# A two-layer hybrid mixer on one core: three memory panels as rounded passes, state-space powers built eight at a time, sines in another order

## The chip, the cores and the metric

One core of one Trainium2 chip runs the whole program. The metric is the device time of one execution in microseconds. Three runs of the kernel before gave 1199.49, 1192.95 and 1200.73 us, a median of 1199.49 us.

## The reference, cut to what matters

The program is a transformer of two layers over 512 tokens of width 1024. Layer 0 mixes with a gated MLP and a state-space model (S5), layer 1 with an mLSTM and block attention; each layer then has cross attention to a memory of 256 rows and a mixture of 16 experts. The change touches only the first tenth: the keys and values of the memory, and the tables of the state-space model.

```python
# memory keys and values: (256 x 1024) @ (1024 x 2048), once for both layers
memn = rmsnorm(mem, mem_norm_g);  kv = memn @ w_mem_kv
# state-space model: 32 groups, 64 complex states, 16 channels a group
lam_bar = exp(lam * step)
b_bar = ((lam_bar - 1.0) / lam)[..., None] * b_mat
bu = einsum('bsgi,gpi->bsgp', u, b_bar)
_, states = associative_scan(_linear_combine, (lam_bar, bu), axis=1)
y = einsum('bsgp,gip->bsgi', states, c_mat).real
```

The kernel cuts the 512 tokens into chunks of 8. It needs the powers lam_bar^0 to lam_bar^8 times B (the table `s5Qn`, 8 powers) and times C (the table `s5PP`, 9 powers), and rotations by sines and cosines (`s5sin`, `s5cos`) of 64 chunk angles for each of 32 groups.

## The kernel before, in words

All tensors stay on chip as 128 partitions by columns. Each engine has its own hand-written queue of instructions; semaphores order them, and nothing else does. A bank of PSUM is claimed, filled and evacuated by counters.

**Weights** come in panels of 1024 x 512 (2 MB) into two slots of SBUF in turn: kv0 to kv3 for the memory, then ev2, ev1 and ev0 of the mixer. `load_panel` on SP's queue waits until the last product of the slot's previous panel is filled.

**Products of two kinds.** `memory_gemm(n)` (line 894) multiplies in full f32: per panel 2 tiles of rows times 8 steps of k, 16 products of 128 x 128 by 128 x 512; the trace records each as two matmuls. `split_gemm` (line 856) splits each factor into a rounded high part and a low rest (type fp32r) and takes three products, high x high, high x low and low x high: 96 matmuls a panel for 4 row tiles. The parts of the weights go through rings of four tiles, `whi` and `wlo`: for each k, ScalarE copies the 128 x 512 tile to `whi` (line 1481), GpSimd subtracts it from the panel to `wlo` (line 686), TensorE uses both and frees the place (`w_used`).

**The stretch that the change touches** on each engine, in queue order:

- TensorE: memory_gemm(0); transposes of C; memory_gemm(1); 32 transposes of x, which wait for `xn_ready` (`transpose_gain_norm("mix_norm0")`, line 829); memory_gemm(2) and (3); 32 transposes of the table s5Qn (line 917), which wait for `s5_tables` 1; the split product ev2; the products `w` (line 929), which wait for `s5_tables` 2; transposes of the memory keys.
- VectorE: the arguments of exponentials and sines (lines 2098 to 2116), a wait for the sines, the powers' magnitudes (2119, 2120), the mean of x (2123), 13 small operations (2126 to 2135), signs of B and C (2137, 2141), x times its reciprocal root (2154), `combine(BB1)`, the low parts of x (2026), `combine(BB2)`, then 8 and 9 calls of `combine` (2147 to 2149: two multiplications and an addition of 128 x 512 each) for the two tables, then the scaling of the memory keys (2169) and the evacuation of `s5u` (2061).
- ScalarE: squares of the memory, the exponentials (1560 to 1563), squares of x (1504, after x has landed), four sines (1567 to 1570), the root of x, evacuations of kv0 and kv1, the high parts of x (1473), squares of the keys (1583), evacuations of kv2 and kv3, the high parts of the first tiles of ev2 (1481).
- GpSimd: constants, then nothing until the low parts of ev2 (686).

Of the kernel before, what the change touches and what calls it, by code (L numbers as in the profile page):

```python
# [22 lines left out]
F32 = mybir.dt.float32  # L23
# [8 lines left out]
P = 128  # L32
# [44 lines left out]
def program(nc, A, out):  # L77
# [19 lines left out]
    with ctx:  # L97
# [74 lines left out]
        names = """x_in rows_in small_in s5_in lam_in zeros_ready s5_b2 rstd_ready consts_ready mem_rstd wide_in mem_in panel0 panel1 x_hi w_hi w_lo w_used  # L172
        stat_ready if_split hmean_ready hstd_ready mean_ready std_ready xn_ready s5_args s5_exp s5_sin s5_tables s5_w s5_t memk_norm
        ln_mean ln_sq vh_ready ws_masked s5_scan s5_x ya_hi gated ya_lo hd_sq max_ready probs mo_probs last_probs sums_ready wt_second diag_rstd qk_scaled
        a_step d_step p_step qk_ready d_norm ml_args ml_act ml_rows diag_ready dt_ready conv_in hh_sq hh_rstd hh_ready
        spare_rows out_stored xs_stored route_rows y_gathered0 y_gathered1 y_gathered2 y_gathered3
        onehots_ready first_ready late_cols late_onehots late_hi late_lo late_filled xs_rows slots_ready table_ready gate_args gate_exp msum_ready""".split()
# [107 lines left out]
        def await_panel(eng, name):  # L285
# [5 lines left out]

        split_panels = ["ev2", "ev1", "ev0"] + ["out00", "out01"] + \
                       [f"{w}0{n}" for w in ("wq", "wo") for n in range(2)] + [f"od{n}" for n in range(7)] + \
# [144 lines left out]
        memtok = v3(E[0], 2, 2048, 4096)  # L438
        memnT = v3(E[0], 8, 0, 2048)
        memKTf = memKT[:, :, :].rearrange("p a b -> p (a b)")  # L440
        headsel = wsT[0:4, :].rearrange("p (h m) -> p h m", h=4)
# [209 lines left out]
        def _(pool):  # L651
# [29 lines left out]
            def low_parts(*names, k0=0, k1=KT):  # L681
                for name in names:
                    for k in range(k0, k1):
                        s_ = step(name, k)
                        pool.wait_ge(S["w_hi"], s_ + 1)
                        pool.tensor_tensor(wlo[s_ % RING][:, :], slot(name)[:, block_of(name, k), :], whi[s_ % RING][:, :].bitcast(F32),  # L686
                                           ALU.subtract).then_inc(S["w_lo"], 1)

            low_parts("ev2")
            low_parts("ev1", k1=RING)  # L690
# [106 lines left out]
        def _(pe):  # L797
# [88 lines left out]
            def memory_gemm(n):  # L886
                await_panel(pe, f"kv{n}")
                for t in range(MT):
# [7 lines left out]
                    fill(ins, u)  # L896

            memory_gemm(0)

            pe.wait_ge(S["s5_in"], 16 * len(s5_loads))  # L900
            for n, c in enumerate((Cst1, Cst2)):
# [4 lines left out]
                fill(ins, u)  # L906
            memory_gemm(1)
            transpose_gain_norm("mix_norm0")
            memory_gemm(2)
            memory_gemm(3)  # L910

# [22 lines left out]
            u = first["memKT"]  # L934
            pe.wait_ge(S["memk_norm"], 1)
            for k in range(0, KT, 2):
# [86 lines left out]
            pe.wait_ge(S["ws_masked"], 1)  # L1023
            pe.wait_ge(S["vh_ready"], 1)
            for n in range(H):
# [297 lines left out]
            claim(pe, u)  # L1323
            pe.wait_ge(S["diag_rstd"], 1)
            for t in range(TT):
# [4 lines left out]
            claim(pe, u)  # L1330
            pe.wait_ge(S["if_split"], 1)
            for k in range(KT):
# [125 lines left out]
        def _(act):  # L1458
# [98 lines left out]
            act.activation(std[:, 0, 0:MT], ssq[:, 0, 0:MT], ACT.Sqrt).then_inc(S["std_ready"], 1)  # L1557

            act.wait_ge(S["s5_in"], 16 * len(s5_loads))
            act.activation(step_, lstep, ACT.Exp).then_inc(S["s5_exp"], 1)  # L1560
            act.wait_ge(S["s5_args"], 1)
            act.activation(mag, mag, ACT.Exp).then_inc(S["s5_exp"], 1)
            act.activation(rho8, are, ACT.Exp, scale=float(LC)).then_inc(S["s5_exp"], 1)
            squares("mix_norm0")
            act.wait_ge(S["s5_args"], 2)
            act.wait_ge(S["consts_ready"], 2)
            act.activation(Li, Li, ACT.Sin, scale=TWO_PI).then_inc(S["s5_sin"], 1)
            act.activation(Lr, Lr, ACT.Sin, bias=halfpi[:, 0:1], scale=-TWO_PI).then_inc(S["s5_sin"], 1)
            act.activation(s5sin, s5sin, ACT.Sin, scale=TWO_PI).then_inc(S["s5_sin"], 1)
            act.activation(s5cos, s5cos, ACT.Sin, bias=halfpi[:, 0:1], scale=-TWO_PI).then_inc(S["s5_sin"], 1)  # L1570
            root("mix_norm0")

            def mem_rstd(n):
                return rstd[:, 0, n:n + 1]

            act.wait_ge(S["mem_rstd"], 1)
            copies("kv0", 0, 2, lambda n: memtok[:, n, 0:512], scale=mem_rstd)
            copies("kv1", 0, 2, lambda n: memtok[:, n, 512:1024], scale=mem_rstd)
            norm("mix_norm0")
            taken(act, first["kv1"] + 1)  # L1580
            for t in range(MT):
# [422 lines left out]
        def _(dve):  # L2004
# [107 lines left out]
            fraction(Li, Lt)  # L2112
            v(stt(Lr, Li, -1.0, Li, ALU.mult, ALU.max))
            v(tt(s5sin, last(t8, NC), mid(iof[:, 0:NC], G), ALU.mult))
            fraction(s5sin, s5cos)
            v(stt(s5cos, s5sin, -1.0, s5sin, ALU.mult, ALU.max), "s5_args")
# [4 lines left out]
            n0 = NORMS["mix_norm0"]  # L2121
            dve.wait_ge(S["stat_ready"], 2 + 4 * n0)
            v(ts(ssq[:, n0, :], ssq[:, n0, :], 1.0 / D, EPS, ALU.mult, ALU.add), "mean_ready")

            lr1, li1 = Lr[:, :, 1], Li[:, :, 1]
# [5 lines left out]
            for dst, a, b, op in ((Fr, nr, li1, ALU.add), (Fi, li1, nr, ALU.subtract)):  # L2131
                v(tt(n1, a, lamr, ALU.mult))
                v(tt(n2, b, lami, ALU.mult))
                v(tt(n1, n1, n2, op))
                v(tt(dst, n1, th, ALU.mult))
            dve.wait_ge(S["s5_b2"], 32)
            v(ts(B2, B2, nsgn[:, 0:1], None, ALU.mult))
# [7 lines left out]
            def combine(dst, p, a, q, b, op=ALU.add):  # L2145
# [3 lines left out]
                v(tt(dst, tA, tB, op))  # L2149

            dve.wait_ge(S["std_ready"], v.n["mean_ready"])
# [3 lines left out]
            combine(BB1, Fr, B1, Fi, B2)  # L2155
            norm("mix_norm0")
            combine(BB2, Fr, B2, Fi, B1, ALU.subtract)
            for j in range(LC):
                combine(s5Qn[:, :, j, :], Lr[:, :, LC - 1 - j], BB1, Li[:, :, LC - 1 - j], BB2)
# [10 lines left out]
            ins.then_inc(S["memk_norm"], 1)  # L2170

# [51 lines left out]
            dve.wait_ge(S["small_in"], 16 * (len(small) + 1))  # L2223
            tt(Gv, Gv, mid(lngain, 4), ALU.mult).then_inc(S["vh_ready"], 1)
            taken_all(dve, "u0", 4)
# [339 lines left out]
            for t in range(TT):  # L2565
                ins = ts(rstd_diag[:, t * P:(t + 1) * P], ident[:], rstd[:, NORMS["mix_norm1"], t:t + 1], None, ALU.mult)
            ins.then_inc(S["diag_rstd"], 1)
# [7 lines left out]
            dve.nop().then_inc(S["if_split"], 1)  # L2575

# [204 lines left out]
```

## Time and profile before

| | |
|---|---|
| median of three runs | 1199.49 us (1192.95 to 1200.73) |
| profiled execution | span 1194.6 us; the page gives no other time for it |
| TensorE matmul busy | 1161.5 us (97%) |
| TensorE weight loads | 869.9 us (73%) |
| VectorE | 705.1 us (59%) |
| ScalarE | 620.6 us (52%) |
| GpSimd | 373.8 us (31%) |

The span counts from the first to the last instruction of the profiled execution. A busy share is an average over the whole span; the stretch of the change is its first 110 us. In the timeline each line has its start, its duration, engine, source line, operation and count, and in brackets the idle time before it and what ended it.

### The profile page before, as it was taken

Reading aid. Unit: us, or ns where it says so; the run is one execution under the profiler, and the core shown is the slowest. Engines: PE = TensorE matmul, PEld = TensorE weight load, DVE = VectorE, ACT = ScalarE, POOL = GpSimd, SP = SyncE. Lnnn points to the kernel's source line nnn. Section 1 sums busy time; section 2 is a strip of 40 time slices with the busy share of each in tenths; the row PEclk is TensorE's granted clock in tenths of the full one; section 3 lists DMA queues with packets and bytes.
Section 4 is the critical chain, followed back from the end, with each engine's and each line's share of the span. In section 5 each row is a group of like instructions: output and inputs, shape, how many; then the busy total and the mean of one; then the engine's idle time right before and its main releaser. Section 6 shows DMA issues by size and latency. Waiting matters only on the chain.

```text
span 1194.6 us, 15606 instructions
## 1 busy us (share of the span) xinstructions
PE 1161.5 (97%) x5302; PEld 869.9 (73%) x5302; DVE 705.1 (59%) x1267; ACT 620.6 (52%) x1190; POOL 373.8 (31%) x342
## 2 busy tenths in 40 slices
PE   8999999999999899999999999989999998999998
PEld 5468876788778567777778887668887785677776
DVE  4797443332332688888645993682323316888886
ACT  2733245446543467777534354444365524677773
POOL 2034340564223031110635754353442130311113
PEclk9999999999999999999999999999999999999999
DMA  9542232279200989998642221022322009799968
GB/s 295 147 141 79 33 115 72 71 260 373 71 1 5 382 322 390 392 375 322 118 148 80 71 77 65 1 71 71 129 83 72 1 1 386 303 395 382 388 267 186
DMA packets 77644, 213.21 MB, mean 178 GB/s; under 512 B 24039, under 2 KB 24979, under 8 KB 65272
## 3 DMA queue, kind: packets, MB, share of 16 engines
q1 hardware_dynamic: 64688, 180.22, 41.0%
q0 software_dynamic: 10048, 27.20, 7.8%
q10 hardware_dynamic: 2840, 4.91, 1.1%
q8 instruction: 40, 0.66, 0.2%
q14 instruction: 28, 0.23, 0.1%
HBM read 187.90 MB, written 32.51 MB: 185 GB/s over the span
## 4 chain that ended last, share of the span: by engine, by line
PE 82%; DMA 5%; DVE 5%; ACT 4%; issue 2%; SPq 1%; POOL 1%; ACTq 0%; DVEq 0%; POOLq 0%
PE bank L856 39%; PE bank L1222 7%; PE bank L1251 7%; PE bank L1217 6%; PE bank L1076 2%; PE bank L1098 2%; PE bank L894 2%; DMA xs<-E 1%; PE bank L829 1%; PE bank L1037 1%; SPq L613 1%; DMA h<-in_x 1%; DVE E2r L2480 1%; DMA ybuf<-E 1%; ACT E2r L1799 1%
## 5 line engine op out<-in xcount | busy, mean ns | idle before, releaser
L686 POOL TENSOR_TENSOR wlo<-W,whi 128x512 fp32r<-128x512 f32 x176 | 256.7, 1479 | 423.1 <-ACT whi L1481 422.7
L1481 ACT ACTIVATE whi<-W 128x512 fp32r<-128x512 f32 x176 | 108.0, 630 | 244.2 <-PE bank L856 222.9
L856 PE MATMUL bank<-whi,xTr 128*128 128x512 f32 x480 | 193.2, 403 | 1.2 <-ACT E L1967 0.6
L856 PE MATMUL bank<-wlo,xTr 128*128 128x512 f32 x416 | 162.8, 391 | 0.0
L856 PEld LDWEIGHTS bank<-whi,xTr 128*128 128x128 f32 x480 | 90.5, 189 | 22.1 <-POOL wlo L686 2.0
L856 PE MATMUL bank<-whi,E4r 128*128 128x512 f32 x256 | 99.8, 390 | 0.0
L1222 PE MATMUL bank<-E4r,E1r 128*128 128x512 f32 x360 | 98.8, 423 | 0.0
L856 PEld LDWEIGHTS bank<-wlo,xTr 128*128 128x128 f32 x416 | 78.7, 189 | 16.7 <-issue 1.2
L2069 DVE TENSOR_TENSOR h<-bank,h 128x512 f32<-128x512 f32 x32 | 21.8, 691 | 115.0 <-PE bank L856 115.0
L1222 PEld LDWEIGHTS bank<-E4r,E1r 128*128 128x128 f32 x360 | 67.6, 188 | 26.9 <-issue 13.4
L1251 PE MATMUL bank<-whi,E2r 128*128 128x512 f32 x240 | 82.8, 406 | 2.2 <-DVE E2r L2480 0.6
L856 PE MATMUL bank<-whi,E0r 128*128 128x512 f32 x160 | 63.7, 398 | 0.0
L856 PE MATMUL bank<-whi,E2r 128*128 128x512 f32 x160 | 62.4, 390 | 0.0
L856 PE MATMUL bank<-wlo,E0r 128*128 128x512 f32 x160 | 62.2, 389 | 0.0
L720 POOL COPY st<-sm 128x1 f32 x24 | 4.3, 181 | 176.9 <-PE bank L1195 176.9
L1251 PEld LDWEIGHTS bank<-whi,E2r 128*128 128x128 f32 x240 | 45.0, 187 | 18.7 <-DVE E2r L2480 9.8
L894 PE MATMUL bank<-W,E 128*128 128x512 f32 x128 | 57.2, 607 | 0.8 <-DMA W<-in_w_mem_kv 0.8
L856 PEld LDWEIGHTS bank<-whi,E4r 128*128 128x128 f32 x256 | 48.1, 188 | 10.1
L723 POOL DMA_INDIRECT E<-xs,idx x30 | 40.9, 1364 | 26.3 <-POOL idx L721 25.1
L894 PEld LDWEIGHTS bank<-W,E 128*128 128x128 f32 x128 | 24.7, 195 | 31.1 <-issue 30.2
L1251 PE MATMUL bank<-wlo,E2r 128*128 128x512 f32 x120 | 46.8, 390 | 0.0
L1775 ACT ACTIVATE E4r<-W 128x512 fp32r<-128x512 f32 x56 | 33.3, 626 | 23.0 <-DVE sm L2445 18.5
(506 smaller groups left out, 2519.2 us busy)
## 6 DMA issues: line engine op xcount, KB each, us to landing
E<-in_moe_w SPq DMA_DIRECT2D x48, 1024.0 KB, 15.5
W<-in_moe_w SPq DMA_DIRECT2D x32, 1024.0 KB, 11.4
xT<-in_moe_w SPq DMA_DIRECT2D x16, 1024.0 KB, 18.8
W<-in_od_w_in SPq DMA_DIRECT2D x7, 2048.0 KB, 8.5
ybuf<-E SPq DMA_DIRECT2D x26, 512.0 KB, 12.5
ybuf<-memV POOLq DMA_DIRECT2D x12, 1024.0 KB, 19.9
W<-in_w_mem_kv SPq DMA_DIRECT2D x4, 2048.0 KB, 8.9
W<-in_xa_wq SPq DMA_DIRECT2D x4, 2048.0 KB, 8.0
```

Of the source, the lines that this page charges most:

```text
L686: pool.tensor_tensor(wlo[s_ % RING][:, :], slot(name)[:, block_of(name, k), :], whi[s_ % RING][:, :].bitcast(F32), ALU.subtract).then_inc( ...
L723: pool.indirect_dma_start(xg[par], None, xs[l], bass.IndirectOffsetOnAxis(ap=idx[:, par:par + 1], axis=0), bounds_check=T - 1, oob_is_err= ...
L856: ins = pe.matmul(bank(u + t)[:, :], a, b, start=(k == 0 and n == 0), stop=(k == KT - 1 and n == 2))
L894: ins = pe.matmul(bank(u)[:, :], memnT[:, k, t * P:(t + 1) * P], slot(f"kv{n}")[:, k, :], start=(k == 0), stop=(k == KT - 1))
L1076: ins = pe.matmul(bank(u)[:, head * NM:(head + 1) * NM], qT[:, k, t * P:(t + 1) * P], memKT[:, k, :], start=(kk == 0), stop=(kk == 1))
L1098: ins = pe.matmul(bank(u)[:, :], memV[:, k, n * XD + d * P:n * XD + (d + 1) * P], pT[:, n, k, :], start=(k == 0), stop=(k == 1))
L1217: pe.matmul(banks[2 + par][:, :], xgT[:, k, :], w13s[j][:, :, k, :], start=(k == 0), stop=False)
L1222: ins = pe.matmul(banks[2 + par][:, :], a, b, start=False, stop=(c == SPLIT - 1 and n == 2))
L1251: ins = pe.matmul(banks[5 + half][:, :], a, b[:, :], start=(k == 0 and n == 0), stop=(k == 1 and n == 2))
L1481: act.activation(whi[s_ % RING][:, :], slot(name)[:, block_of(name, k), :], ACT.Copy).then_inc(S["w_hi"], 1)
L1775: act.activation(up_hi[c].rearrange("p (n f) -> p n f", n=2), w13s[nj][:, :, KT - SPLIT + c, :], ACT.Copy)\
L2069: evac(tt(hs, bank(u)[:, :], hs, ALU.add), u)
```

## The change

It does five things.

1. Panels kv1, kv2 and kv3 are multiplied as three rounded passes (`memory_split`): 48 matmuls a panel, in steps of k, through the same rings. kv0 stays as it was. The normed memory is split once: ScalarE copies 128 x 2048 to `mem_hi`, GpSimd subtracts to `mem_lo`. Both lie in the buffer E5, where s5PP is built later.
2. ScalarE's queue gets the 24 high parts of these panels between its other work, and GpSimd's queue the 24 low parts ahead of those of ev2.
3. The tables: `combine_eight` builds eight powers with three operations of 128 x 4096 in place of 24 of 128 x 512; the ninth power of s5PP stays a `combine`. The second call waits until kv3's banks are filled.
4. The powers' sines come right after their arguments. The rotation's arguments (`s5sin`, `s5cos`) are finished by VectorE after the 13 small operations, and ScalarE takes their sines after the evacuations of `bT`.
5. VectorE takes the mean of x after the signs of B and C, and `combine(BB1)` before the scaling of x. Some semaphores are merged (`even_setup`, `odd_setup`), with the same order of waits.

```diff
-        split_panels = ["ev2", "ev1", "ev0"] + ["out00", "out01"] + \
+        split_panels = ["kv1", "kv2", "kv3", "ev2", "ev1", "ev0"] + ["out00", "out01"] + \
...
+        mem_hi, mem_lo = v3(E5r, 8, 0, 2048), v3(E5r, 8, 2048, 4096)
...
-            low_parts("ev2")
+            pool.wait_ge(S["mem_hi"], 1)
+            pool.tensor_tensor(mem_lo, memnT, mem_hi.bitcast(F32), ALU.subtract).then_inc(S["mem_lo"], 1)
+            low_parts("kv1", "kv2", "kv3", "ev2")
...
+            def memory_split(n):
+                for k in range(KT):
+                    s_ = step(f"kv{n}", k)
+                    pe.wait_ge(S["w_lo"], s_ + 1)
+                    wh, wl = whi[s_ % RING], wlo[s_ % RING]
+                    for t in range(MT):
...
+                        for i, (a, b) in enumerate(((mem_hi[:, k, c], wh), (mem_hi[:, k, c], wl), (mem_lo[:, k, c], wh))):
+                            ins = pe.matmul(bank(u)[:, :], a, b[:, :], start=(k == 0 and i == 0),
+                                            stop=(k == KT - 1 and i == 2))
...
+                    if k < KT - 1:
+                        ins.then_inc(S["w_used"], 1)
...
-            memory_gemm(1)
+            pe.wait_ge(S["mem_lo"], 1)
+            memory_split(1)
             transpose_gain_norm("mix_norm0")
-            memory_gemm(2)
-            memory_gemm(3)
+            memory_split(2)
+            memory_split(3)
...
+            act.activation(mem_hi, memnT, ACT.Copy).then_inc(S["mem_hi"], 1)
             act.wait_ge(S["s5_in"], 16 * len(s5_loads))
             act.activation(step_, lstep, ACT.Exp).then_inc(S["s5_exp"], 1)
...
-            squares("mix_norm0")
...
+            weights("kv1", 0, RING)
+            act.wait_ge(S["mem_rstd"], 1)
+            copies("kv0", 0, 2, lambda n: memtok[:, n, 0:512], scale=mem_rstd)
+            squares("mix_norm0", 0, 2)
+            weights("kv1", RING, RING + 2)
+            squares("mix_norm0", 2, 4)
+            weights("kv1", RING + 2, KT)
+            root("mix_norm0")
+            weights("kv2", 0, RING - 1)
+            copies("kv1", 0, 2, lambda n: memtok[:, n, 512:1024], scale=mem_rstd)
+            weights("kv2", RING - 1, RING)
+            norm("mix_norm0")
+            weights("kv2", RING, RING + 1)
+            taken(act, first["kv1"] + 1)
+            weights("kv2", RING + 1, RING + 2)
+            memory_key_squares(0)
+            weights("kv2", RING + 2, RING + 3)
+            memory_key_squares(1)
+            weights("kv2", RING + 3, KT)
+            weights("kv3", 0, RING)
             copies("kv2", 0, 2, lambda n: memV[:, n, 0:512], scale=mem_rstd)
-            weights("ev2", 0, RING)
+            weights_between("kv3", "ev2")
             copies("kv3", 0, 2, lambda n: memV[:, n, 512:1024], scale=mem_rstd)
...
+            act.wait_ge(S["s5_args"], 3)
+            act.activation(s5sin, s5sin, ACT.Sin, scale=TWO_PI).then_inc(S["s5_sin"], 1)
+            act.activation(s5cos, s5cos, ACT.Sin, bias=halfpi[:, 0:1], scale=-TWO_PI).then_inc(S["s5_sin"], 1)
...
+            def combine_eight(dst, p, a, q, b):
+                def over_eight(x):
+                    return x.unsqueeze(2).broadcast_to([P, G, LC, GI])
+                product = hflat.rearrange("p (g j i) -> p g j i", g=G, j=LC)
+                tt(dst, last(p, GI), over_eight(a), ALU.mult)
+                v(tt(product, last(q, GI), over_eight(b), ALU.mult))
+                v(tt(dst, dst, product, ALU.add))
+
+            combine_eight(s5Qn, Lr[:, :, LC - 1::-1], BB1, Li[:, :, LC - 1::-1], BB2)
             dve.nop().then_inc(S["s5_tables"], 1)
-            for k in range(LC + 1):
-                combine(s5PP[:, :, k, :], Lr[:, :, k], C1, Li[:, :, k], C2)
+            for t in range(MT):
+                await_filled(dve, first["kv3"] + t)
+            combine_eight(s5PP[:, :, 0:LC, :], Lr[:, :, 0:LC], C1, Li[:, :, 0:LC], C2)
+            combine(s5PP[:, :, LC, :], Lr[:, :, LC], C1, Li[:, :, LC], C2)
             dve.nop().then_inc(S["s5_tables"], 1)
```

## Rows read from the trace of the kernel before

**Rows 1.** The page, busy time of the engines.

```profile
PE 1161.5 (97%) x5302; PEld 869.9 (73%) x5302; DVE 705.1 (59%) x1267; ACT 620.6 (52%) x1190; POOL 373.8 (31%) x342
```

**Rows 2.** Chain of waits, 0 to 260 us: start, duration in us, engine, output, line.

```profile
46.04 5.05 PE bank L829 x29
51.09 27.47 PE bank L894 x64
78.56 3.49 PE bank L917 x32
82.05 21.82 PE bank L856 x96
...
108.51 3.67 PE bank L929 x32
```

**Rows 3.** Timeline of TensorE, 26 to 52 us: start, duration, in brackets idle time.

```profile
28.47 13.90 PE L894 MATMUL bank<-W,E 128*128 128x512 f32 x32
44.14 0.30 PE L829 MATMUL bank<-ident,h 128*128 128x128 f32 x1 [1.78 <-DVE h L2154]
```

**Rows 4.** Timeline of VectorE, 10 to 48 us.

```profile
17.43 0.19 DVE L2098 TENSOR_TENSOR sm<-sm 128x32 f32<-128x32 f32 x1 [2.34 <-ACT sm L1560]
...
21.02 0.46 DVE L2113 SCALAR_TENSOR_TENSOR memKT<-memKT 128x288 f32<-128x288 f32 x1
21.51 2.29 DVE L2114 TENSOR_TENSOR E<-sm,iof 128x2048 f32<-128x2048 f32 x1
23.84 1.23 DVE L2103 TENSOR_SCALAR E<-E 128x2048 f32<-128x2048 f32 x1
...
37.87 0.19 DVE L2126 TENSOR_SCALAR sm<-memKT 128x32 f32<-128x32 f32 x1
...
41.00 0.49 DVE L2137 TENSOR_SCALAR E<-E,nsgn 128x512 f32<-128x512 f32 x1
...
43.24 2.74 DVE L2154 TENSOR_SCALAR h<-h,rstd 128x1024 f32<-128x1024 f32 x4
```

**Rows 5.** Timeline of ScalarE, 14 to 40 us.

```profile
17.07 0.23 ACT L1560 ACTIVATE sm<-sm 128x32 f32<-128x32 f32 x1 [1.34 <-DMA E<-in_s_c_re]
...
30.11 1.06 ACT L1504 ACTIVATE memV<-h 128x1024 f32<-128x1024 f32 x1 [9.86 <-DMA h<-in_x]
...
36.46 1.89 ACT L1569 ACTIVATE E<-E 128x2048 f32<-128x2048 f32 x1
```

**Rows 6.** Timelines of VectorE and GpSimd, 72 to 101 us.

```profile
72.42 0.68 DVE L2148 TENSOR_TENSOR E<-memKT,E 128x512 f32<-128x512 f32 x1
...
73.86 1.65 DVE L2147 TENSOR_TENSOR E<-memKT,E 128x512 f32<-128x512 f32 x1
...
99.59 1.03 DVE L2017 TENSOR_SCALAR st<-st 128x8 f32<-128x8 f32 x1
...
73.48 6.51 POOL L686 TENSOR_TENSOR wlo<-W,whi 128x512 fp32r<-128x512 f32 x4 [62.14 <-ACT whi L1481]
```

**Rows 7.** Timelines of VectorE and GpSimd, 141 to 155 us; last row: line 686, min/median/max ns.

```profile
141.14 2.29 DVE L2195 TENSOR_TENSOR h<-h 128x2048 f32<-128x2048 f32 x1
141.43 3.17 POOL L686 TENSOR_TENSOR wlo<-W,whi 128x512 fp32r<-128x512 f32 x1 [3.60 <-ACT whi L1481]
...
145.90 5.21 DVE L2199 TENSOR_TENSOR_SCAN E<-E,h 128x2048 f32<-128x2048 f32 x1
151.15 3.21 DVE L2200 TENSOR_TENSOR h<-E 128x2048 f32<-128x2048 f32 x1
...
L686 POOL TENSOR_TENSOR wlo<-W,whi x176: 1262/1292/5272, 73.5 to 975.1; 128x512 fp32r<-128x512 f32 x176
```

**Rows 8.** The page, DMA issues: size, median us from issue to landing.

```profile
W<-in_w_mem_kv SPq DMA_DIRECT2D x4, 2048.0 KB, 8.9
```

**Rows 9.** Windows of TensorE: stretch, busy (count), granted clock, DMA.

```profile
46.00:48.00 2.00, 1.96 (x10) 0.54 1.05 406
48.00:50.00 2.00, 2.00 (x13) 0.60 1.12 319
```

More of the change, by code:

```diff
@@ L172, in program @@
         names = """x_in rows_in small_in s5_in lam_in zeros_ready s5_b2 rstd_ready consts_ready mem_rstd wide_in mem_in panel0 panel1 x_hi w_hi w_lo w_used
-        stat_ready if_split hmean_ready hstd_ready mean_ready std_ready xn_ready s5_args s5_exp s5_sin s5_tables s5_w s5_t memk_norm
-        ln_mean ln_sq vh_ready ws_masked s5_scan s5_x ya_hi gated ya_lo hd_sq max_ready probs mo_probs last_probs sums_ready wt_second diag_rstd qk_scaled
+        stat_ready hmean_ready hstd_ready mean_ready std_ready xn_ready s5_args s5_exp s5_sin s5_tables s5_w s5_t even_setup
+        ln_mean ln_sq ws_masked s5_scan s5_x ya_hi gated ya_lo hd_sq max_ready probs mo_probs last_probs sums_ready wt_second odd_setup qk_scaled
         a_step d_step p_step qk_ready d_norm ml_args ml_act ml_rows diag_ready dt_ready conv_in hh_sq hh_rstd hh_ready
+        mem_hi mem_lo
         spare_rows out_stored xs_stored route_rows y_gathered0 y_gathered1 y_gathered2 y_gathered3
@@ L896, in memory_gemm @@
                     fill(ins, u)
+            def memory_split(n):
[4 more added lines that the diff above has]
+                    for t in range(MT):
+                        u = first[f"kv{n}"] + t
+                        if k == 0:
+                            claim(pe, u)
+                        c = slice(t * P, (t + 1) * P)
+                        for i, (a, b) in enumerate(((mem_hi[:, k, c], wh), (mem_hi[:, k, c], wl), (mem_lo[:, k, c], wh))):
+                            ins = pe.matmul(bank(u)[:, :], a, b[:, :], start=(k == 0 and i == 0),
+                                            stop=(k == KT - 1 and i == 2))
+                        if k == KT - 1:
+                            fill(ins, u)
+                    if k < KT - 1:
+                        ins.then_inc(S["w_used"], 1)
             memory_gemm(0)
@@ L934, in _ @@
             u = first["memKT"]
-            pe.wait_ge(S["memk_norm"], 1)
+            pe.wait_ge(S["even_setup"], 1)
             for k in range(0, KT, 2):
@@ L1023, in _ @@
             pe.wait_ge(S["ws_masked"], 1)
-            pe.wait_ge(S["vh_ready"], 1)
+            pe.wait_ge(S["even_setup"], 2)
             for n in range(H):
@@ L1323, in _ @@
             claim(pe, u)
-            pe.wait_ge(S["diag_rstd"], 1)
+            pe.wait_ge(S["odd_setup"], 1)
             for t in range(TT):
@@ L1330, in _ @@
             claim(pe, u)
-            pe.wait_ge(S["if_split"], 1)
+            pe.wait_ge(S["odd_setup"], 2)
             for k in range(KT):
@@ L1557, in _ @@
             act.activation(std[:, 0, 0:MT], ssq[:, 0, 0:MT], ACT.Sqrt).then_inc(S["std_ready"], 1)
+            taken(act, first["memT"] + 2)
+            taken(act, first["memT"] + 3)
+            act.activation(mem_hi, memnT, ACT.Copy).then_inc(S["mem_hi"], 1)
             act.wait_ge(S["s5_in"], 16 * len(s5_loads))
@@ L1568, in _, with memory_key_squares @@
             act.activation(Lr, Lr, ACT.Sin, bias=halfpi[:, 0:1], scale=-TWO_PI).then_inc(S["s5_sin"], 1)
-            act.activation(s5sin, s5sin, ACT.Sin, scale=TWO_PI).then_inc(S["s5_sin"], 1)
-            act.activation(s5cos, s5cos, ACT.Sin, bias=halfpi[:, 0:1], scale=-TWO_PI).then_inc(S["s5_sin"], 1)
-            root("mix_norm0")
             def mem_rstd(n):
                 return rstd[:, 0, n:n + 1]
[L1576 to L1581, printed above, removed]
+            def memory_key_squares(t):
                 for n in range(4):
@@ L2112, in _ @@
             fraction(Li, Lt)
-            v(stt(Lr, Li, -1.0, Li, ALU.mult, ALU.max))
+            v(stt(Lr, Li, -1.0, Li, ALU.mult, ALU.max), "s5_args")
             v(tt(s5sin, last(t8, NC), mid(iof[:, 0:NC], G), ALU.mult))
-            fraction(s5sin, s5cos)
-            v(stt(s5cos, s5sin, -1.0, s5sin, ALU.mult, ALU.max), "s5_args")
             dve.wait_ge(S["s5_exp"], 3)
@@ L2120, in _ @@
             v(tt(Li, Li, mag, ALU.mult))
-            n0 = NORMS["mix_norm0"]
-            dve.wait_ge(S["stat_ready"], 2 + 4 * n0)
-            v(ts(ssq[:, n0, :], ssq[:, n0, :], 1.0 / D, EPS, ALU.mult, ALU.add), "mean_ready")
             lr1, li1 = Lr[:, :, 1], Li[:, :, 1]
@@ L2135, in _ @@
                 v(tt(dst, n1, th, ALU.mult))
+            fraction(s5sin, s5cos)
+            v(stt(s5cos, s5sin, -1.0, s5sin, ALU.mult, ALU.max), "s5_args")
             dve.wait_ge(S["s5_b2"], 32)
@@ L2149, in combine @@
                 v(tt(dst, tA, tB, op))
+            n0 = NORMS["mix_norm0"]
+            dve.wait_ge(S["stat_ready"], 2 + 4 * n0)
+            v(ts(ssq[:, n0, :], ssq[:, n0, :], 1.0 / D, EPS, ALU.mult, ALU.add), "mean_ready")
+            combine(BB1, Fr, B1, Fi, B2)
             dve.wait_ge(S["std_ready"], v.n["mean_ready"])
@@ L2154, in _ @@
                 ts(h[:, t, :], h[:, t, :], rstd[:, NORMS["mix_norm0"], t:t + 1], None, ALU.mult).then_inc(S["xn_ready"], 1)
-            combine(BB1, Fr, B1, Fi, B2)
+            combine(BB2, Fr, B2, Fi, B1, ALU.subtract)
             norm("mix_norm0")
-            combine(BB2, Fr, B2, Fi, B1, ALU.subtract)
-            for j in range(LC):
-                combine(s5Qn[:, :, j, :], Lr[:, :, LC - 1 - j], BB1, Li[:, :, LC - 1 - j], BB2)
+            def combine_eight(dst, p, a, q, b):
[6 more added lines that the diff above has]
+            combine_eight(s5Qn, Lr[:, :, LC - 1::-1], BB1, Li[:, :, LC - 1::-1], BB2)
             dve.nop().then_inc(S["s5_tables"], 1)
-            for k in range(LC + 1):
-                combine(s5PP[:, :, k, :], Lr[:, :, k], C1, Li[:, :, k], C2)
+            for t in range(MT):
+                await_filled(dve, first["kv3"] + t)
+            combine_eight(s5PP[:, :, 0:LC, :], Lr[:, :, 0:LC], C1, Li[:, :, 0:LC], C2)
+            combine(s5PP[:, :, LC, :], Lr[:, :, LC], C1, Li[:, :, LC], C2)
             dve.nop().then_inc(S["s5_tables"], 1)
@@ L2169, in _ @@
                 ins = ts(k, k, xrec[:, n:n + 1], None, ALU.mult)
-            ins.then_inc(S["memk_norm"], 1)
+            ins.then_inc(S["even_setup"], 1)
             copies("s5u", 0, 4, lambda n: uT[:, n, :])
@@ L2223, in _ @@
             dve.wait_ge(S["small_in"], 16 * (len(small) + 1))
-            tt(Gv, Gv, mid(lngain, 4), ALU.mult).then_inc(S["vh_ready"], 1)
+            tt(Gv, Gv, mid(lngain, 4), ALU.mult).then_inc(S["even_setup"], 1)
             taken_all(dve, "u0", 4)
@@ L2566, in _ @@
                 ins = ts(rstd_diag[:, t * P:(t + 1) * P], ident[:], rstd[:, NORMS["mix_norm1"], t:t + 1], None, ALU.mult)
-            ins.then_inc(S["diag_rstd"], 1)
+            ins.then_inc(S["odd_setup"], 1)
             v(dve.memset(VML[:, :, :, P:P + 1], 1.0))
@@ L2574, in _ @@
                 v(tt(iflo[:, :, 32 * n:32 * n + 4], w_, hi_.bitcast(F32), ALU.subtract))
-            dve.nop().then_inc(S["if_split"], 1)
+            dve.nop().then_inc(S["odd_setup"], 1)
             dve.wait_ge(S["rows_in"], 16 * (len(rows_loads) - 1 + len(rope_loads)))
```

## The prediction, made before the changed kernel ran

> **What bounds the kernel now.** I read the page first: TensorE is busy for 97% of the span [rows 1], so a change counts by what it takes from or gives to TensorE's queue. The chain of waits over the first 260 us shows whose work that is here. From 46 us it is TensorE without a gap that matters: transposes of x to 51.1, two full f32 panels in 27.47 us, 32 transposes, and ev2's 96 matmuls in 21.82 us, to 103.9 us [rows 2]. After that it follows TensorE again. What ev2's end moves, the rest of the span moves by.
>
> Before 46 us TensorE's timeline has one idle place: kv1 ends at 42.4, and the transposes wait for VectorE's scaled x, 1.78 us and then piece by piece [rows 3]. VectorE scales x at 43.24 to 45.98 [rows 4], so the chain of small operations ahead of it is the second bound.
>
> The third view is GpSimd against VectorE, because the change gives GpSimd 24 more low parts and a big one. A 128 x 512 operation on VectorE takes 0.68 us alone and 1.65 while GpSimd subtracts, and one of 8 columns then takes 1.03; four low parts take 6.51 us, 1.63 each [rows 6]. So a low part costs VectorE 0.97 us. The reverse is dearer: behind a 2.29 us operation a low part took 3.17 us, and the longest of all, 5272 ns, lies behind the 5.21 us scan, against a median of 1292; the next 128 x 2048 operation then took 3.21 us and not 2.29 [rows 7]. The two engines take strict turns, instruction by instruction.
>
> **The change part by part.**
>
> *Products.* Three passes of 96 matmuls cost 21.82 us [rows 2], 0.227 each; 48 cost 10.9 us against 13.90 for an f32 panel [rows 3]: 3.0 less, 9 us for three. A step of k takes 6 x 0.227 = 1.36 us, and GpSimd alone needs 1.29 (the median) [rows 7], so it just keeps up if VectorE leaves it alone.
>
> *VectorE's chain to scaled x, without GpSimd.* ScalarE's copy to mem_hi costs 1.9 us (as 128 x 2048 sine) [rows 5] and delays the first exponential from 17.07 to 17.7: +0.6. So the powers' arguments end at 22.1 (21.48 before [rows 4]). Then the s5sin product 2.3, two multiplications 1.0, 13 small operations 3.1 (37.87 to 41.00), the rotation's fraction and absolute value 1.23 + 2 x 2.29 = 5.9 with gaps, B and C 2.0 (41.00 to 43.0), the mean 0.2, BB1 2.0, scaling 2.8 [rows 4]: 41.4 us against 45.98. The squares are no limit: x lands at 30.1 [rows 5], four squares and two high parts end near 35.5.
>
> *With GpSimd.* mem_lo is four low parts long. It starts near 16.4 and I take 4 x 1.0 us; VectorE's first operation wants to start at 17.9 and waits: +2.8. The eight low parts of kv1 (panel issued at 15.2, landed near 24 by [rows 8]) fall on the continuous chain, +7.8. The root stands ahead of kv2's high parts in ScalarE's queue, so kv2's first four low parts begin just as BB1 and the scaling run: +3.9. Scaled x is complete at 55.9, 10 us later than before. kv1 ends near 40.5, TensorE idles 15 us, and the transposes end 5.1 us after scaled x (as 45.98 to 51.09), at 61.0.
>
> *kv2 and kv3.* Four tiles are ready, two more come while VectorE reads PSUM (its low parts of x, about 57 to 63; one operand in SBUF). Then BB2 (2.1, plus two turns) to about 66.5, and three operations of 128 x 4096 for s5Qn. Their length is not in the trace: 2 x 2.29 less one fixed part of 0.15 = 4.43 us. Bounds are 4.3 and 5.5 (eight times 0.69). With a low part in each gap it is 3 x 4.43 + 2 x 0.97, to 82. kv2's last two tiles come in those gaps, near 72 and 77, and kv2 ends at 78.7 (64.8 before). kv3's eight low parts find a free port only after s5Qn: 82.7 + 7 x 1.29 + 1.36, kv3 ends at 93.5 against 78.56: +15. The tables' own saving (24 x 0.69 = 16.5 against 13.3) is worth nothing, since TensorE never waited for s5Qn.
>
> *s5PP* now cannot start before kv3 ends. It takes 13.3 + 2.1 + five turns of 0.97 = 20.2, to 114. TensorE has 3.5 us of transposes and ev2 as cover, 97.2 to 119 at best. But ev2's third, fourth and fifth low parts wait out these operations (to about 99.6, 105.0 and 110.4), where TensorE needs one each 2.72 us. That costs it 2.3 us: ev2 ends at 121.3, not 103.87: **+17.4**. The later sines (3.9 us and a table load, in ScalarE's queue ahead of ev2's fifth high part) end near 104.6; ahead of the fifth low part, they hide. So does the panel ev2: issued at kv2's end, landed 9 us later, first used by ScalarE after 90. SP's other loads wait for nothing new. The key squares end before VectorE needs them. The products w then need 8.3 us as before, the keys' scaling being bound by the root behind ev1's fourth high part in both.
>
> The Trainium skill, "SBUF — State Buffer", section "Who interferes with whom", speaks against this change: a VectorE instruction with two SBUF inputs, and a GpSimd one that reads SBUF, hold the shared port for the whole instruction. By it the 4.43 us operations block a low part completely, and the sum stays +17.4; without it the sum would be the second rival's. The 5272 ns row agrees; no row read here has a VectorE operand of 4096 columns.
>
> **Sum.** The profiled span of 1194.6 becomes 1212.0. The median of the runs stood 4.9 us above that span, so 1216.9; I say 1217. With a turn at 0.8 us the same laying out gives +13, at 1.2 us +25.
>
> **Rivals.**
>
> *Half-rate clock.* After the 1.78 us gap the granted clock was 0.54 and 0.60 for four microseconds [rows 9], 1.2 GHz for most of it. After 15 us idle and starved steps in kv2, kv3 may begin at that level: its steps of 1.36 become 2.7 for three or four steps, and the same for ev2's starved start: +4 to +8 on top, 1221 to 1225. For it: such a gap did it here. Against: kv2 and ev2 wait for GpSimd anyway. Chance 0.1.
>
> *No blocking that counts (other side).* If long broadcast operations leave gaps for GpSimd, or the chain's small operations pass it, TensorE sets the pace: scaled x at 41.4, transposes done at 46.4 (-4.7), kv2 and kv3 in 22.4 us and not 27.5 (-5.1): -9.8, ev2 ends at 94 and the median becomes 1189.7. It decides if a low part beside a 4.43 us operation takes under 1.6 us. Against it stand all rows of 6 and 7. A further 3 us could come from the stall before w and full-clock transposes, 1186.5. Chances 0.2 and 0.08.
>
> *Lighter turns.* The turn is 0.5 us, since many of VectorE's operations in the chain are of 0.2 us and GpSimd's read ends before its record: the same laying out gives +7, 1206; +3 to +11 with the big operations at either bound. Chance 0.17.
>
> *mem_lo* could cost four whole median records, 5.2 us [rows 7], and not four turns; another 1.3 us then falls on VectorE, inside the main range.
>
> **How the numbers follow.** The main case (+12 to +22, 1211.5 to 1222) has 0.45, the clock 0.1, lighter turns 0.17, no blocking 0.2, more than that 0.08. One per cent, 12 us, is about what can be told from no change. Slower by over 1%: 0.45 + 0.1 = 0.55. Within: 0.17 + 0.2 = 0.37. Faster: 0.08. The range reaches from the no-blocking case, 1189, to 1224; it leaves out some 0.1 on either side. The main case's own range is 1211 to 1224.
>
> **What would show it.** Low parts (line 686) of 5 to 5.5 us beside the first table's three operations, and again in ev2. VectorE's small operations near 1.2 us where GpSimd works. A first transpose of x behind an idle gap of over 10 us, transposes done near 61, kv3 near 93, ev2 near 121. I am wrong if the low parts stay near 1.3 to 1.6 us throughout, if scaled x is complete before 46, or if kv3 ends before 80.

## The result, and the profile after

The change made the kernel slower: a median of 1213.66 us (4 runs, 1211.61 to 1215.15) against 1197.83 us (4 runs), ratio 1.0163, 95% interval 1.0138 to 1.0188, which is +16.5 to +22.5 us. The four runs of the kernel before taken beside it give only 15.8 us, a quotient of 1.0132 that lies below this interval; the ratio 1.0163 puts the kernel before at 1194.2 us, and its later runs, 7 to 29 at a time, have medians of 1194.0 to 1195.4. I go by the ratio. The profiled execution has a span of 1209.8 us, 15.2 more than before. The page's first line, which answers to [rows 1]:

```profile
PE 1155.5 (96%) x5350; PEld 878.2 (73%) x5350; DVE 710.3 (59%) x1225; ACT 637.9 (53%) x1217; POOL 435.3 (36%) x367
```

TensorE is busy 6 us less and the profiled span is 15 us longer. The chain of waits (start, duration, engine, output, line), which answers to [rows 2]:

```profile
50.45 5.43 DVE h L2195 x4
55.92 5.51 PE bank L833 x29
...
63.63 16.02 POOL wlo L688 x3
79.70 15.53 PE bank L913 x60
...
106.64 5.10 POOL wlo L688
111.88 11.18 PE bank L860 x48
...
128.42 3.67 PE bank L952 x32
...
157.86 19.05 PE bank L860 x84
```

Before, TensorE alone made the chain from 46 us on. Now VectorE's scaling of x takes 5.43 us instead of 2.74 [rows 4] and ends 9.9 us later; the transposes end at 61.4 instead of 51.1; GpSimd's low parts hold the chain for 16 us in kv2 and 5 in ev2; ev2 ends at 123.1 instead of 103.9, and w's second half starts at 128.42 instead of 108.51. I use one mark for every run below: the start of the 84 matmuls of ev1, the first long stretch of products behind everything that the change touches. It is 157.86 here and 137.95 before: +19.9 us.

GpSimd and VectorE beside the first table (timelines, GpSimd's three rows from narrow windows):

```profile
63.63 5.21 POOL L688 TENSOR_TENSOR wlo<-W,whi 128x512 fp32r<-128x512 f32 x1 [8.97 <-ACT whi L1504]
68.81 5.44 POOL L688 TENSOR_TENSOR wlo<-W,whi 128x512 fp32r<-128x512 f32 x1
74.20 5.44 POOL L688 TENSOR_TENSOR wlo<-W,whi 128x512 fp32r<-128x512 f32 x1
...
63.30 4.41 DVE L2205 TENSOR_TENSOR E<-memKT,E 128x4096 f32<-128x4096 f32 x1
67.64 5.49 DVE L2206 TENSOR_TENSOR h<-memKT,E 128x4096 f32<-128x4096 f32 x1
73.16 5.37 DVE L2207 TENSOR_TENSOR E<-E,h 128x4096 f32<-128x4096 f32 x1
```

A *turn* is here the time for which one engine holds the other. Of the 5.2 to 5.4 us of a low part (1.29 us alone) about 1.1 is left once the VectorE operation that it met has ended: the first ends 1.1 us behind the operation of 63.30, and so on. VectorE's next operation is longer by the same turn, 5.49 and 5.37 against 4.41. TensorE's timeline shows who paid, in brackets:

```profile
52.01 0.45 PE L833 MATMUL bank<-ident,h 128*128 128x128 f32 x1 [12.14 <-DVE h L2195]
...
68.89 0.50 PE L913 MATMUL bank<-whi,E5r 128*128 128x512 f32 x1 [1.99 <-POOL wlo L688]
...
74.30 0.79 PE L913 MATMUL bank<-whi,E5r 128*128 128x512 f32 x1 [3.73 <-POOL wlo L688]
...
79.70 0.50 PE L913 MATMUL bank<-whi,E5r 128*128 128x512 f32 x1 [2.48 <-POOL wlo L688]
```

Of the 19.9 us at the mark the profiled span shows 15.2, because the rest of the program was 4.7 us shorter in this execution. Chains of waits, the same two places in the kernel before and, second fence, after:

```profile
303.17 5.46 PE bank L856 x24
...
1181.14 9.08 PE bank L1274 x40
```

```profile
323.06 5.46 PE bank L860 x24
...
1196.41 9.08 PE bank L1297 x40
```

That is 878.0 us between the two rows before and 873.4 after. The same stretch took 873.0, 875.3, 872.5 and 875.7 us in the first four experiments, which share this code: it varies by itself, and before was the longest. Part of the difference in this pair is one panel's transfer, 9.12 against 7.87 us on the chain. So I read nothing as given back; the interval of the repeated runs holds 19.9.

### The profile page after: what moved, and what is told of

It is laid out like the page before. It is cut to its first block, busy times and chain, and to the rows that moved or that the text cites. A ratio compares the mean times of both kernels' runs of the same rounds, so it can differ in the third digit from the quotient of the medians.

```text
span 1209.8 us, 15724 instructions
## 1 busy us (share of the span) xinstructions
PE 1155.5 (96%) x5350; PEld 878.2 (73%) x5350; DVE 710.3 (59%) x1225; ACT 637.9 (53%) x1217; POOL 435.3 (36%) x367
## 4 chain that ended last, share of the span: by engine, by line
PE 80%; DVE 7%; ACT 5%; DMA 4%; POOL 2%; issue 1%; ACTq 0%; DVEq 0%; POOLq 0%
PE bank L860 38%; PE bank L1274 8%; PE bank L1245 8%; PE bank L1240 6%; DMA xs<-E 3%; PE bank L1099 2%; PE bank L1121 2%; POOL wlo L688 2%; PE bank L1297 2%; ACT E L1796 1%; PE bank L913 1%; PE bank L1060 1%; DVE E2r L2532 1%; PE bank L833 1%; ACT E2r L1840 1%
## 5 line engine op out<-in xcount | busy, mean ns | idle before, releaser
L688 POOL TENSOR_TENSOR wlo<-W,whi 128x512 fp32r<-128x512 f32 x200 | 312.4, 1576 | 376.2 <-ACT whi L1504 375.5
L1504 ACT ACTIVATE whi<-W 128x512 fp32r<-128x512 f32 x200 | 122.5, 630 | 250.2 <-PE bank L860 223.1
L860 PEld LDWEIGHTS bank<-wlo,xTr 128*128 128x128 f32 x416 | 78.2, 188 | 16.5 <-issue 1.2
L1274 PE MATMUL bank<-whi,E2r 128*128 128x512 f32 x240 | 82.7, 405 | 2.2 <-DVE E2r L2532 0.6
L727 POOL DMA_INDIRECT E<-xs,idx x30 | 41.4, 1379 | 25.8 <-POOL idx L725 25.8
L1816 ACT ACTIVATE E4r<-W 128x512 fp32r<-128x512 f32 x56 | 33.3, 627 | 21.8 <-DVE sm L2497 17.4
L1240 PE MATMUL bank<-E 128*128 128x512 f32 x96 | 43.8, 592 | 0.0
L2385 DVE TENSOR_TENSOR E<-bank,fgain 128x512 f32<-128x512 f32 x64 | 41.2, 682 | 4.3 <-PE bank L1218 2.1
## 6 DMA issues: line engine op xcount, KB each, us to landing
E<-in_moe_w SPq DMA_DIRECT2D x48, 1024.0 KB, 15.2
xT<-in_moe_w SPq DMA_DIRECT2D x16, 1024.0 KB, 17.4
```

What stands on the lines that cost most here:

```text
L727: pool.indirect_dma_start(xg[par], None, xs[l], bass.IndirectOffsetOnAxis(ap=idx[:, par:par + 1], axis=0), bounds_check=T - 1, oob_is_err= ...
L860: ins = pe.matmul(bank(u + t)[:, :], a, b, start=(k == 0 and n == 0), stop=(k == KT - 1 and n == 2))
L1240: pe.matmul(banks[2 + par][:, :], xgT[:, k, :], w13s[j][:, :, k, :], start=(k == 0), stop=False)
L1274: ins = pe.matmul(banks[5 + half][:, :], a, b[:, :], start=(k == 0 and n == 0), stop=(k == 1 and n == 2))
L1504: act.activation(whi[s_ % RING][:, :], slot(name)[:, block_of(name, k), :], ACT.Copy).then_inc(S["w_hi"], 1)
L1816: act.activation(up_hi[c].rearrange("p (n f) -> p n f", n=2), w13s[nj][:, :, KT - SPLIT + c, :], ACT.Copy)\
```

## The experiments

The theory, *turns*: a subtraction on GpSimd and a VectorE operation that both read SBUF (two operands, or a scaling of SBUF data) do not overlap. A low part costs VectorE about 1 us; a VectorE operation costs a low part its whole length. A low part is the subtraction that makes the rest of a weight tile. Rivals: the feed of the passes (rings, ScalarE's order), the clock, the new order on VectorE, the long operations alone. Each ratio is to the runs of the kernel before that belong to that experiment (medians 1193.96 to 1195.41). The mark is that of one profiled execution, so it moves with the clock of that execution too.

| run | median us | ratio to before (95%) | mark us |
|---|---|---|---|
| before | 1194 to 1198 | 1 | 137.95 |
| the change | 1213.66 | 1.0163 (1.0138 to 1.0188) | 157.86 |
| no passes | 1190.42 | 0.9975 (0.9946 to 1.0004) | 140.01 |
| single powers | 1214.77 | 1.0168 (1.0136 to 1.0199) | 159.99 |
| GpSimd writes only | 1188.20 | 0.9947 (0.9929 to 0.9964) | 135.31 |
| the order alone | 1186.96 | 0.9942 (0.9926 to 0.9959) | 132.83 |
| s5u evacuated first | 1187.50 | 0.9943 (0.9921 to 0.9964) | 131.60 |
| twelve dummies | 1199.79 | 1.0043 (1.0024 to 1.0062) | 148.27 |
| eight powers alone | 1194.74 | 0.9995 (0.9979 to 1.0011) | 141.89 |
| kv3 alone | 1197.82 | 1.0023 (1.0007 to 1.0039) | 140.62 |
| free chain | 1203.66 | 1.0075 (1.0049 to 1.0101) | 147.85 |

**No passes.**

```diff
-            memory_split(1)
+            memory_gemm(1)
...
-            low_parts("kv1", "kv2", "kv3", "ev2")
+            low_parts("ev2")
...
-            for t in range(MT):
-                await_filled(dve, first["kv3"] + t)
             combine_eight(s5PP[:, :, 0:LC, :], Lr[:, :, 0:LC], C1, Li[:, :, 0:LC], C2)
```

> The change without the rounded passes: kv1 to kv3 as full f32 panels again, no high or low parts for them, no split of the memory; the sines' order, the mean's place and the tables built eight at a time stay, and the second table no longer waits for kv3. Turns theory (each low part takes about 1 us from VectorE, each VectorE operation with two SBUF operands holds a low part back for its whole length): the loss is gone, scaled x is complete near 40, the transposes start when kv1 ends (42.4) and end near 47 instead of 51; the first table is off the path; about 4 us faster than the kernel before, median near 1194. Rival, the order (the mean behind the rotation's arguments and the signs costs the gain): scaled x at 46 or later, 1198 to 1201.

Measured 1190.42 us, where 1194 was expected; the loss is gone, and the ratio's interval just reaches no change. Its ten runs spread from 1185.88 to 1198.14, with a mean granted clock of 0.999 in the fastest and 0.988 in the slowest. The profiled one, 1195.07, shows one stretch at the lower rate (chain of waits, then windows of TensorE: busy, granted clock):

```profile
42.50 3.49 PE bank L831 x32
45.99 27.47 PE bank L896 x64
...
117.28 12.55 PE bank L1001 x64
```

```profile
116.00:118.00 2.00, 1.58 (x18) 1.00 0.26 27
118.00:120.00 2.00, 2.00 (x14) 0.67 0.74 90
120.00:122.00 2.00, 2.00 (x12) 0.50 0.76 101
```

The transposes start at 42.5 without a wait and end at 46.0 (expected 47). The 64 small products of V, a step of the state-space model, ran at a granted clock of 0.50, 1.2 GHz: 12.55 us and not 7.29 as in the kernel before, and what follows at that rate costs another 1.2. So 6.5 us of this mark are the clock's.

**Single powers.**

```diff
-            combine_eight(s5Qn, Lr[:, :, LC - 1::-1], BB1, Li[:, :, LC - 1::-1], BB2)
+            for j in range(LC):
+                combine(s5Qn[:, :, j, :], Lr[:, :, LC - 1 - j], BB1, Li[:, :, LC - 1 - j], BB2)
```

> The change with both tables built by single powers again (27 more operations of 128x512 in place of six of 128x4096), all else as changed. Turns theory: low parts no longer wait 5.4 us, kv3 ends near 86 instead of 95, but each of the 24 short operations now pays a turn, the first table is ready only near 96 and the second near 121; the products w start as late as in the change, median 1212 to 1215. Rival, the long operations alone are the loss: with short ones it falls to 1197 to 1202.

Measured 1214.77. GpSimd, VectorE and the chain:

```profile
71.41 22.09 POOL L688 TENSOR_TENSOR wlo<-W,whi 128x512 fp32r<-128x512 f32 x13 [1.34 <-ACT whi L1504]
```

```profile
82.16 1.77 DVE L2185 TENSOR_TENSOR E<-memKT,E 128x512 f32<-128x512 f32 x1
83.97 1.67 DVE L2186 TENSOR_TENSOR E<-E 128x512 f32<-128x512 f32 x1
```

```profile
96.94 6.47 PE bank L940 x32
```

Low parts take 1.70 us each, 22.09 / 13, TensorE is fed (kv3 ends at 88.5, 86 expected), and the first table is ready at 96.9 as forecast (96). The price moved from TensorE's feed to the table. The long operations by themselves are not the loss: with either length the two engines' turns add up to the same delay.

**GpSimd writes only.**

```diff
-            pool.tensor_tensor(mem_lo, memnT, mem_hi.bitcast(F32), ALU.subtract).then_inc(S["mem_lo"], 1)
-            low_parts("kv1", "kv2", "kv3", "ev2")
+            pool.memset(E5r[:, 2048:4096].bitcast(F32), 0.0).then_inc(S["mem_lo"], 1)
+            for name in ("kv1", "kv2", "kv3"):
...
+                    pool.memset(wlo[s_ % RING][:, :].bitcast(F32), 0.0).then_inc(S["w_lo"], 1)
+            low_parts("ev2")
```

> The change with GpSimd writing zeros in place of the low parts of the memory and of kv1 to kv3 (the low parts of this product are left out; everything is multiplied as before, ev2 and later panels are complete). GpSimd then reads no SBUF there. Turns theory: the 128x512 and 128x4096 operations of VectorE with two SBUF operands are not held; scaled x near 41 to 43, kv3 ends near 69, ev2 near 96, 7 to 9 us faster than the kernel before, median near 1190. Rival, the feed through ScalarE, the clock or the queue order is the loss: kv3 ends after 85 and the median stays above 1205.

Measured 1188.20, 6 us below before (7 to 9 expected), and 25 below the change, with the same matmuls, the same ScalarE queue and the same waits. VectorE's long operations (timeline), then the chain:

```profile
50.80 4.41 DVE L2210 TENSOR_TENSOR E<-memKT,E 128x4096 f32<-128x4096 f32 x1
55.13 4.42 DVE L2211 TENSOR_TENSOR h<-memKT,E 128x4096 f32<-128x4096 f32 x1
59.58 4.43 DVE L2212 TENSOR_TENSOR E<-E,h 128x4096 f32<-128x4096 f32 x1
```

```profile
43.35 5.58 PE bank L838 x29
48.92 22.11 PE bank L918 x96
...
82.46 5.15 POOL wlo L688
```

4.42 us and not 5.4; kv2 and kv3 in 22.1 us. So the loss is GpSimd's reads of SBUF against VectorE's. The Trainium skill, "SBUF — State Buffer", section "Who interferes with whom", has this distinction: an operation with two SBUF inputs collides with a GpSimd instruction that reads SBUF, not with one that only writes. The rows agree, 5.4 us beside subtractions and 4.42 beside memsets. The feed and the order as causes fall. A memset is also shorter (0.52 us), so this run shows what the loss is tied to, not that writes are free: VectorE's scaling of x took 3.08 us beside memsets against 2.74, and a scaling of 128 x 512 took 0.92 against 0.49. The miss lies in places that the edit left alone: kv3 ended at 71.0 (69 expected), in part because the transposes ran at half rate (5.58 us), and ev2 at 100.5 (96), since its own low parts still met the second table, 5.15 us of one on the chain.

**The order alone.** The edit of the run without passes and that of the single powers together: the kernel before in the new order (and with the merged semaphores).

> The kernel before with nothing but the new order (powers' sines first, rotation's arguments and sines late, mean and first combine moved): full f32 panels and single powers. Turns theory: the tables' length is off TensorE's path both ways, so this equals the run without the passes within 1 us, median near 1194. Rival, building eight at a time carries a gain: 3 us or more slower than that run.

Measured 1186.96, the fastest, 0.6% below before; expected was 1194.

```profile
39.02 2.75 DVE h L2179 x4
41.82 3.39 PE bank L831 x29
45.21 27.47 PE bank L896 x64
```

Scaled x is complete at 41.8, and the transposes, with 0.34 us of idle time before them, run at the full clock: 3.39 us and not 5.05 as in [rows 2]. This second gain stood in the prediction only as a part of the 3 us of its best case. The tables' form adds nothing that these runs can tell: the run without passes differs from this one by its half-rate V products and otherwise by 0.8 us, because its kv1 ended at 42.5 and not at 40.7 (kv0, the same code, took 15.70 us there and 14.00 here).

**s5u evacuated first.**

```diff
-            rstd_of(xmx[:, 0:8], xnm[:, 0:8], xrec[:, 0:8], XD, "hmean_ready", "hstd_ready")
+            rstd_of(xmx[:, 0:8], xnm[:, 0:8], xrec[:, 0:8], XD, "hmean_ready", "hstd_ready", None,
+                    lambda: copies("s5u", 0, 4, lambda n: uT[:, n, :]))
```

> The order alone, with one more step moved: VectorE evacuates s5u between the keys' mean and the wait for their root, so the second half of the products w no longer waits 1.06 us for it. Expected: w's second half starts about 1 us earlier, 5.5 to 8 us faster than the kernel before, median near 1186. If something else is late there (the keys' scaling before their transposes), the gain over the order alone is 0.

```profile
98.68 7.09 PE bank L949 x64
```

The products w run through: they end 7.1 us after ev2 and not 9.0. As ev2 itself ended 0.7 us later in this execution, the mark is 1.2 us earlier. The ratio, 0.9943, lies in the 5.5 to 8 us that were expected, but so does that of the order alone: the medians (1187.50 and 1186.96) don't resolve the step.

**Twelve dummies.**

```diff
+            pool.wait_ge(S["s5_exp"], 3)
+            for i in range(12):
+                w_ = wlo[i % RING][:, :]
+                p_(pool.tensor_tensor(w_, w_.bitcast(F32), w_.bitcast(F32), ALU.subtract))
             low_parts("ev2")
```

> The order alone, and GpSimd, idle there, makes twelve subtractions of 128x512 on its own ring, which nobody reads, right after the powers' exponentials; the panels stay full f32 products. Turns theory: each costs VectorE's chain about 0.97 us, scaled x is complete near 53 instead of 41.8, the transposes end near 57 instead of 45.2, 11 us slower than the order alone, median near 1198. Rival, the change's late x comes from the feed of its passes: no difference, median near 1187.

Measured 1199.79, 12.8 us above the order alone. GpSimd, and VectorE's small operations (0.19 us alone) beside it:

```profile
20.42 15.93 POOL L696 TENSOR_TENSOR wlo<-wlo 128x512 fp32r<-128x512 f32 x12 [6.64 <-ACT sm L1589]
```

```profile
28.49 0.91 DVE L2151 TENSOR_SCALAR sm<-memKT 128x32 f32<-128x32 f32 x1
29.43 0.19 DVE L2152 TENSOR_TENSOR sm<-sm 128x32 f32<-128x32 f32 x1
29.66 0.92 DVE L2153 TENSOR_TENSOR sm<-sm 128x32 f32<-128x32 f32 x1
...
46.84 2.75 DVE h L2185 x4
```

Work that nobody waits for makes x late by 7.8 us (49.6 against 41.8, 53 expected): 0.65 a dummy, not 0.97. Two things show in the rows. Some operations of 0.19 us pass unheld. And a dummy holds for less than a low part: VectorE's operations of 0.46 us became 1.18 to 1.23 beside dummies and 1.42 to 1.44 beside the change's low parts, 0.72 to 0.77 more against 0.96 to 0.98. A dummy reads one tile twice and waits for the dummy before it; which of the two makes it lighter was not tested.

The mark is 15.4 us later than in the order alone: 7.8 by late x, 1.2 by transposes at half rate (4.61 us against 3.39), 6.4 by V at half rate here too (12.23 us) and what follows it. But this was one of the three slowest of ten executions (1204.09), and how much of the median's 12.8 us is the clock was not seen.

**Eight powers alone.** The kernel before with `combine_eight` for both tables.

> The kernel before with both tables built eight powers at a time and nothing else. Turns theory: the first table ends near 69 and was never waited for; in the second the first four low parts of ev2 meet the long operations and take about 5 us each, but TensorE needs them only from 82 on. Within 1 us of the kernel before, median 1193 to 1196. Rival, starvation reaches ev2: 3 us or more slower; rival, the tables carry a gain: 3 us or more faster.

Measured 1194.74, ratio 0.9995. The second table's operations took 4.42, 5.49 and 5.39 us, seven low parts of ev2 19.71 us, 2.8 each, and TensorE went through ev2 in 21.82 us. A starved feed with enough lead costs nothing. The mark, 3.9 us later than before, holds 6.5 us of half-rate V and what follows; up to there this execution was 2.5 us ahead, with x landed earlier and the transposes at full clock (3.38 us).

**kv3 alone.** The order alone, with memory_split(3), its high and low parts, and the memory's split beside VectorE's reads of PSUM.

> The order alone, with kv3 by itself as three rounded passes (single powers; the memory split after the chain to scaled x, beside VectorE's reads of PSUM). TensorE's kv3 ends 3 us earlier, near 70. Turns theory: eight more turns in the first table, ready near 74, so the transposes of it start 1 us later than in the order alone; the second table starts there and ends near 101, 3 us after ev2's end: 1 to 5 us slower than the order alone. Rival, one panel's turns hide: 3 us faster than the order alone, median near 1184.

```profile
61.08 13.30 POOL L688 TENSOR_TENSOR wlo<-W,whi 128x512 fp32r<-128x512 f32 x8 [1.55 <-ACT whi L1505]
```

```profile
44.02 5.36 DVE E1r L2059 x8
...
77.83 6.16 PE bank L941 x32
```

Measured 1197.82, 10.9 above the order alone, twice the 1 to 5 expected; the mark shows 7.8 of it, and the other 3 us were not found. The first table is ready at 77.8, not 74: the first four low parts of ev2 follow at once and add their turns, and the transposes behind the gap ran at half rate (6.16 us against 3.49). One panel's turns don't hide either. The memory's subtraction ran on GpSimd from 44.63 to 49.19 beside eight of VectorE's operations that read PSUM and one tile of SBUF: they took 5.36 us, as in the order alone, where GpSimd was idle. So the loss isn't GpSimd's work beside any VectorE work.

**Free chain.** As GpSimd writes only, but for the memory and kv1 alone.

> The change with zeros written in place of the low parts of the memory and of kv1 alone (these low parts are left out); kv2, kv3 and ev2 have theirs as in the change. It cuts the loss in two: the chain to scaled x is free of the first twelve turns' worth, the two tables are not. Turns theory: scaled x is complete near 46 (the first four low parts of kv2 still fall on it), the transposes end near 51.5, the low parts beside the tables still take over 5 us, kv3 ends near 85 and ev2 near 113; about 10 us faster than the change, median near 1204. Rival, the tables' starvation is the whole loss: median 1210 or more; rival, the late x is the whole loss: 1196 or less.

```profile
40.48 5.44 DVE h L2199 x4
45.97 5.45 PE bank L837 x29
53.60 16.04 POOL wlo L688 x3
69.69 15.56 PE bank L917 x60
```

Measured 1203.66 (1204). Scaled x at 45.9 (46), kv3's end 85.3 (85), ev2's 113.1 (113); the mark is 10.0 us earlier than in the change, and the 16 us of low parts on the chain are unchanged. Against GpSimd writes only the mark is 12.5 us later, and 2.5 of these are still late x (transposes done at 51.4 against 48.9, by kv2's first four low parts). So of the 22.5 us between that run and the change some 12.5 are late x and 10 are the two tables.

## Why the prediction was right

Forecast 1217 against 1213.66, by the steps it named. The mechanism came as laid out; that the total is within 3.4 us is in part luck. The loss at the mark was 19.9 us and not 17.4 (+2.5), the rest of the program was 4.7 us shorter in the profiled execution, and the median stood 3.9 us above its span and not 4.9. The 4.9 was not a cost of its own: the profiled execution's time is 1.8 us above its span, and the rest is where the median of three runs happened to fall. The range, 1189 to 1224, also took in the cases of no blocking and of lighter turns, so it is the rows that decide and not the number.

- *Turns.* Right: 5.21 to 5.44 us for low parts beside the long operations (5 to 5.5 forecast), and small operations of 1.22 us.
- *The chain.* Scaled x complete at 55.9 (55.9), kv1 ended at 39.9 (40.5), transposes at 61.4 (61.0). The copy to mem_hi took 1.89 us, mem_lo 4.50 on GpSimd (4.0); VectorE's first operation waited 2.78 (2.8). That 2.8 did not follow from its own terms, 16.4 + 4.0 - 17.9 = 2.5.
- *Products.* 9 us less was forecast for TensorE, the page shows 6.0. At the full clock kv2 and kv3 take 22.1 us against 27.5 (GpSimd writes only), and kv1 took 11.4 against 13.9, 7.9 less together; 2.4 us more went in stretches at half rate (below).
- *kv2* was wrong by 5 us: it ended near 84 (ScalarE's copy that waits for it starts at 84.30), not 78.7. I had BB2 behind the low parts of x; in the changed code it stands ahead of them. So s5Qn began at 63.3 and not 66.5, 0.3 us before kv2's fifth low part, which I had taken as free, and three tiles waited where I had two. Half-rate steps followed the gaps (the clock, below).
- *kv3* ended at 95.2 (93.5), because its low parts were ready while TensorE was late with kv2: an error in one term, absorbed by the next. (The sum as written, 82.7 + 7 x 1.29 + 1.36, gives 93.1.)
- *s5PP and ev2.* Second table 115.7 (114), ev2's fifth low part at 111.7 (110.4), ev2's end 123.1 (121.3): +19.2, not +17.4.
- *After ev2* I had 8.3 us for w as before. It lost 0.7 more: ScalarE's root of the keys now follows sines, and a table load of 1.28 us stands in front of it; before, that table was already loaded (the root began at 104.43, at once).
- *Half-rate clock* as a rival was partly true. Windows of TensorE after:

```profile
56.00:58.00 2.00, 2.00 (x10) 0.50 0.00 0
...
82.00:84.00 2.00, 2.00 (x6) 0.50 0.03 8
84.00:86.00 2.00, 2.00 (x10) 0.95 0.28 29
```

  Where TensorE was on the chain it cost 2.4 us beyond the laying out: 0.4 in the transposes (5.51 us against the 5.1 I had, itself partly at half rate) and 1.9 in the sixty matmuls from 79.70 (15.53 us against 60 x 0.227 = 13.6). That is less than the +4 to +8 I gave it, since the waits for low parts covered the rest.
- *No blocking* and *lighter turns* fell. With the reads of the new low parts removed the kernel came to 1188.2, where the first of them had 1189.7; that is a coincidence, as it was a gain of 6.0 us on 1194.2 and not of 9.8 on 1199.5. Lighter turns, 0.65 us, came with the twelve dummies, but the change's own chain lost 14 us (scaled x at 55.9 against 41.8 with the order alone), as laid out.

What I undersold is the order: by itself it is worth 5 us at the mark and 0.6% of the time. In the prediction it stands as 41.4 against 45.98 and, without blocking, 4.7 us; the clock of the transposes behind it has no price of its own.

## What to carry to other kernels

Before giving an idle engine work, ask what memory it reads, and lay its instructions against the other engine's, one by one. Here an idle GpSimd beside a busy VectorE was not spare time: TensorE, relieved of 6 us of matmuls, was 20 us late. Longer instructions saved VectorE some 3 us a table, and no run shows that in the time (eight powers alone: 0.9995), since nothing waited for it. When a change bundles parts, run each alone: the order of a few small operations was the gain here (1186.96 us, the best version found, ratio 0.9942), and the large part cost 25 us at the mark (157.86 against 132.83).

## What the runs showed of the hardware that was not expected

- The 64 products of V (128 x 64) ran in 7.3 us in some executions and 12.2 to 12.6 in others of like code (no passes, eight powers alone, twelve dummies), with the granted clock at 0.50 for most of it. With what follows at that rate it is about 6.5 us, and it can make about half of the spread of single runs from 1186 to 1198 us in one kernel. What starts it was not settled. Each time a short idle stretch stands before it (1.56 to 1.58 of 2 us busy, as in the windows above), but the kernel before, the order alone, s5u evacuated first and kv3 alone had the same stretch (1.57 to 1.59 of 2 us) and ran on at full clock.
- kv0, the first product, is the same code in all of these: it took 14.00 us in the order alone, 15.64 before and 17.01 in eight powers alone, where the granted clock was 0.50 for its first 6 us.
- The transposes of x behind an idle gap of 1.8 to 12 us took 4.6 to 5.6 us; those with at most 0.34 us of idle time before them took 3.4 to 3.5.
